# Last output tile of a projection in its own PSUM bank, squares of the other tiles summed early and folded to 256 columns

## What is computed

```python
def rms_norm(x, g):
    y = xf * lax.rsqrt(jnp.mean(xf * xf, axis=-1, keepdims=True) + EPS)
    return (y * g).astype(x.dtype)

x = x + rms_norm(y, attn_post_g[layer])     # y is the output of w_o (layers 0 and 1)
h = rms_norm(x, ffn_pre_g[layer])
f = swiglu(h, w_gate, w_up, w_down)
x = x + rms_norm(f, ffn_post_g[layer])
...
mod = silu(c) @ w_ada + b_ada               # third layer: six vectors of 1024
x = x + gt_m * mixed                        # then rms_norm(x, g_ffn), modulated
x = x + gt_f * y                            # then the final rms_norm
```

## Time and profile before

| what | value |
|---|---|
| median of 3 runs | 1028.64 us (1028.03 to 1035.65) |
| the profiled execution's own time | 1028.55 us |
| its span, first to last instruction | 1026.4 us |
| mean granted clock of PE | 0.992 of full |

### The profile page before, as it was taken

The page is one execution under the profiler, slowest core; times in us unless marked ns, Lnnn a source line. Parts: engine busy times, 40 slices in busy tenths (PEclk is TensorE's granted clock), DMA queues, the critical chain, the costliest instruction groups (busy, mean ns, idle before and its releaser), DMA issues.

```text
span 1026.4 us, 18901 instructions
## 1 busy us (share of the span) xinstructions
PE 979.2 (95%) x8022; PEld 941.3 (92%) x8022; DVE 710.8 (69%) x1248; ACT 530.1 (52%) x805; POOL 16.4 (2%) x48
## 2 busy tenths in 40 slices
PE   6978999999999999899999999998999999999996
PEld 6968989999998987789999999897999999999996
DVE  5946587787648776688867766546553877878753
ACT  6634474444337455464434443546665456666631
POOL 0000000000000000000000000000120000000000
PEclk9999999999999999999999999999999999999998
DMA  7432556667753733347775873453333544555541
GB/s 278 175 123 83 205 219 235 245 237 259 281 209 129 283 124 123 125 169 285 260 265 202 340 289 121 173 197 121 120 131 123 198 152 155 196 185 186 174 155 42
DMA packets 28307, 194.19 MB, mean 189 GB/s; under 512 B 3264, under 2 KB 3520, under 8 KB 5312
## 3 DMA queue, kind: packets, MB, share of 16 engines
q1 hardware_dynamic: 28224, 192.99, 51.9%
HBM read 191.93 MB, written 1.05 MB: 188 GB/s over the span
## 4 chain that ended last, share of the span: by engine, by line
PE 64%; DVE 17%; ACT 14%; issue 3%; DMA 1%; SPq 1%; POOL 0%; DVEq 0%; ACTq 0%
PE bank L479 17%; PE bank L480 17%; PE bank L481 17%; ACT s_whi L851 7%; DVE s_wlo L1245 4%; DVE s_tmp L1703 2%; PE bank L599 2%; DVE s_tmp L1705 2%; PE bank L524 2%; PE bank L525 1%; PE bank L530 1%; PE bank L579 1%; ACT s_tmp L1205 1%; ACT s_tmp L1201 1%; ACT s_S L895 1%
## 5 line engine op out<-in xcount | busy, mean ns | idle before, releaser
L1245 DVE TENSOR_TENSOR s_wlo<-s_raw,s_whi 128x512 fp32r<-128x512 f32 (+1 forms) x352 | 370.4, 1092 | 160.8 <-ACT s_whi L851 160.6
L851 ACT ACTIVATE s_whi<-s_raw 128x1024 fp32r<-128x1024 f32 (+2 forms) x223 | 303.1, 1387 | 237.0 <-PE bank L481 218.6
L479 PE MATMUL bank<-s_hh,s_whi 128*128 128x256 f32 x1400 | 394.5, 282 | 5.9 <-DVE s_wlo L1245 3.5
L480 PE MATMUL bank<-s_hl,s_whi 128*128 128x256 f32 x1400 | 389.2, 278 | 0.0
L481 PE MATMUL bank<-s_hh,s_wlo 128*128 128x256 f32 x1400 | 389.1, 278 | 0.0
L479 PEld LDWEIGHTS bank<-s_hh,s_whi 128*128 128x128 f32 x1400 | 263.8, 188 | 12.6 <-issue 8.6
L481 PEld LDWEIGHTS bank<-s_hh,s_wlo 128*128 128x128 f32 x1400 | 264.4, 189 | 0.0
L480 PEld LDWEIGHTS bank<-s_hl,s_whi 128*128 128x128 f32 x1400 | 264.0, 189 | 0.1
L479 PE MATMUL bank<-s_ph,s_whi 128*128 128x256 f32 x528 | 147.0, 278 | 0.6 <-DVE s_wlo L1245 0.6
L481 PE MATMUL bank<-s_ph,s_wlo 128*128 128x256 f32 x528 | 146.9, 278 | 0.0
L480 PE MATMUL bank<-s_pl,s_whi 128*128 128x256 f32 x528 | 146.9, 278 | 0.0
(11 more groups left out here) (202 smaller groups left out, 1278.2 us busy)
## 6 DMA issues: line engine op xcount, KB each, us to landing
s_raw<-in_gu SPq DMA_DIRECT2D x44, 1024.0 KB, 4.9
s_raw<-in_dn SPq DMA_DIRECT2D x33, 1024.0 KB, 4.8
s_raw<-in_wada SPq DMA_DIRECT2D x24, 1024.0 KB, 5.3
s_raw<-in_up SPq DMA_DIRECT2D x22, 1024.0 KB, 4.8
s_raw<-in_wo SPq DMA_DIRECT2D x8, 1024.0 KB, 4.8
s_raw<-in_win_g SPq DMA_DIRECT2D x8, 1024.0 KB, 4.7
s_raw<-in_wkv_v SPq DMA_DIRECT2D x4, 1024.0 KB, 5.9
s_raw<-in_wkv_k SPq DMA_DIRECT2D x4, 1024.0 KB, 4.8
```

The source lines that it names most:

```text
L479: e.matmul(out, hi, xh[:, k, :], start=first, stop=False, skip_group_check=True)
L480: e.matmul(out, hi, xl[:, k, :], start=False, stop=False, skip_group_check=True)
L851: e.activation(whi[w % SPLIT][:, at], raw[p % RAW][:, at], ACT.Copy).then_inc(S.hi.tick((w, c0)), 1)
L1245: e.tensor_tensor(wlo[s][:, at], raw[p % RAW][:, at], whi[s][:, at].bitcast(F32), ALU.subtract).then_inc(S.lo.tick((i, j), (i, "all")), 1)
```

## The change

Three things change.

1. `tiles` takes a bank `seven`. In four calls (`dn0` and `dn1` in `feed_forward` with bank 7, `wout` with bank 3, `dn2` with bank 5) the last output tile, number 7, goes to the first half of that bank; tile 6 stays in the old one and gets an event of its own, "six". ACT squares tile 6 and tile 7 in instructions of 128x256 (`last_squares`), DVE adds the squares of tile 6 to the accumulator, and at x5 and x6 it also does the gated add of tile 6 on "six".
2. DVE adds the two halves of the accumulator (`fold`, 128x256), so that PE needs one call over it and not two. With tile 6 in the accumulator, only tile 7 is late: one call, not two.
3. At y0 and y1, which get no bank of their own, PE sums the late pair first (two calls) and the folded accumulator behind it (one call).

`sums("x4")` gives the same eight calls as before, and `ada_sums(0, 7)`, `ada_sums(2, 7)` and the `keep_warm` calls are not edited. The core of the diff:

```diff
+        def tile_out(name, j):
+            if j == 7 and (name, "seven") in bank_of:
+                return banks[bank_of[name, "seven"]][:, 0:T]
+            return banks[bank_of[name, j - j % 2]][:, (j % 2) * T:(j % 2 + 1) * T]
...
-            def tiles(name, n, m, nk, xh, xl, made, b, by, last=0):
+            def tiles(name, n, m, nk, xh, xl, made, b, by, last=0, seven=None):
                 out = take(b, by, (name, n + last))
+                outs = [out[:, j * T:(j + 1) * T] for j in range(m)]
                 bank_of[name, n] = b
+                if seven is not None:
+                    outs[1] = take(seven, by, (name, n + last))[:, 0:T]
+                    bank_of[name, "seven"] = seven
...
+                        event = (name, n) if j == m - 1 else (name, "six") if seven is not None else None
...
+                if acc and s not in ("y0", "y1"):
+                    summed()
+                    for half in range(acc):
...
                 for i, src in late:
                     q.wait_ge(S.square, (s, i))
...
+                    m = e.matmul(out[:, 0:T], ones[:, :], src, start=first, stop=True, skip_group_check=True)
+                    first = False
+                if s in ("y0", "y1"):
+                    summed()
+                    m = e.matmul(out[:, 0:T], ones[:, :], sq[:, 0:T], start=False, stop=True, skip_group_check=True)
...
                 for n in (2, 4, 6):
-                    tiles(d, n, 2, NF, ph[layer], pl[layer], f"p{layer}", n // 2, S.resid, 1)
-                sums(f"z{layer}", 4, late=[(3, sq_late)])
+                    tiles(d, n, 2, NF, ph[layer], pl[layer], f"p{layer}", n // 2, S.resid, 1, 7 if n == 6 else None)
+                sums(f"z{layer}", 4, late=[(3, sq_late[:, 1, :])], acc=1)
...
+            def last_squares(s, j, src, into):
+                if j == 0 and ("sq", into) in sq_free:
+                    q.wait_ge(*sq_free["sq", into])
+                sq_free["sq", into] = (S.sums, s)
+                e.activation(sqb[into][:, j, :], src, ACT.Square).then_inc(S.square.tick((s, ("six", 3)[j])), 1)
...
+            def fold(s):
+                acc = sqacc[ACC_OF[s]]
+                q.wait_latest(S.sqsum)
+                e.tensor_tensor(acc[:, 0:T], acc[:, 0:T], acc[:, T:2 * T], ALU.add).then_inc(
+                    S.sqsum.tick((s, "sum")), 1)
...
+                    if t == 160:
+                        fold(s)
+                        square_sum(s, "six", sqb[3][:, 0, :], T)
...
             def add_gated(name, s, n, gate0):
                 for j in range(2):
+                    if j == 1 or n < 6:
+                        q.wait_ge(S.gemm, (name, n))
+                    else:
+                        q.wait_ge(S.gemm, (name, "six"))
...
+                    elif n == 6:
+                        i.then_inc(S.resid.tick((s, "six")), 1)
+                        fold(s)
+                        square_sum(s, "six", sqb[1][:, 0, :], T)
```

More of the change, by code:

```diff
@@ L545, in tokens, with sums, summed @@
                         token_low(name, g, nk, xl, k, tb)
[L547 removed]
+            def sums(s, b, late=(), acc=2, columns=False):
                 out = take(b, S.act_tmp, ("log", s))
                 bank_of["sums", s] = b
[L551 to L553 removed]
+                sq, first = sqacc[ACC_OF.get(s, 0)], True
+                def summed():
                     q.wait_ge(S.square, (s, 0))
@@ L684, in tensor_program @@
                     values("o0", A0, i, P, A0.PT[i % 2], ("wuv", i // 2, 1), S.soft, ("o0", "turned", i, 1), 7)
-            sums("y0", 4, late=[(3, sqb[1])])
+            sums("y0", 4, late=[(3, sqb[1][:, j, :]) for j in range(2)])
             keep_warm(8, 7)
@@ L743, in tensor_program @@
                     values("o1", A1, i, 64, A1.PT[i % 2], ("wkv_v", i // 4, 1), S.soft, ("o1", "turned", i, 1), 7)
-            sums("y1", 4, late=[(3, sqb[1])])
+            sums("y1", 4, late=[(3, sqb[1][:, j, :]) for j in range(2)])
             keep_warm(8, 7)
@@ L748, in tensor_program @@
             keep_warm(12, 6)
-            sums("x4", 5, late=[(i, sqb[i]) for i in range(4)], acc=False)
+            sums("x4", 5, late=[(i, sqb[i][:, j, :]) for i in range(4) for j in range(2)], acc=0)
             keep_warm(6, 6)
@@ L812, in tensor_program @@
             for n in (4, 6):
-                tiles("wout", n, 2, 8, hh, hl, "mix", (6, 7)[n // 2 - 2], S.resid)
-            sums("x5", 0, late=[(3, sqb[1])])
+                tiles("wout", n, 2, 8, hh, hl, "mix", (6, 7)[n // 2 - 2], S.resid, seven=3 if n == 6 else None)
+            sums("x5", 0, late=[(3, sqb[1][:, 1, :])], acc=1)
             keep_warm(7, 3)
@@ L828, in tensor_program @@
             for n in (2, 4, 6):
-                tiles("dn2", n, 2, NF, ph[2], pl[2], "p2", n // 2, S.resid)
-            sums("x6", 4, late=[(3, sqb[1])])
+                tiles("dn2", n, 2, NF, ph[2], pl[2], "p2", n // 2, S.resid, seven=5 if n == 6 else None)
+            sums("x6", 4, late=[(3, sqb[1][:, 1, :])], acc=1)
         def scalar_program(e, counted):
@@ L935, in y_squares @@
                         square(s, 0, bank[:, :], None, (S.sums, s))
-                    elif i < 3:
+                    else:
                         square(s, i, pair(bank), ring[i - 1], (S.sqsum, (s, i)))
-                    else:
-                        square(s, 3, pair(bank), ring[2], (S.sums, s))
                     yield i
+                if (name, "seven") not in bank_of:
+                    q.wait_ge(S.gemm, (name, 6))
+                    square(s, 3, pair(banks[bank_of[name, 6]]), ring[2], (S.sums, s))
+                else:
+                    for j, done in ((0, "six"), (1, 6)):
+                        q.wait_ge(S.gemm, (name, done))
+                        last_squares(s, j, tile_out(name, 6 + j), ring[2])
+                        yield 3
+            def last_squares(s, j, src, into):
[3 more added lines that the diff above has]
+                e.activation(sqb[into][:, j, :], src, ACT.Square).then_inc(S.square.tick((s, ("six", 3)[j])), 1)
             def x_squares(s, ring):
@@ L1170, in x_pair_squares @@
             def x_pair_squares(s, i, ring):
[L1171 to L1174, removed]
-                else:
-                    square(s, i, src, ring[i - 1], (S.sums, s) if i == 3 else (S.sqsum, (s, i)))
+                if i < 3:
+                    q.wait_ge(S.resid, (s, 2 * i))
+                    src = xT[:, 2 * i:2 * i + 2, :]
+                    square(s, i, src, *((None, (S.sums, s)) if i == 0 else (ring[i - 1], (S.sqsum, (s, i)))))
+                else:
+                    for j, done in ((0, "six"), (1, 6)):
+                        q.wait_ge(S.resid, (s, done))
+                        last_squares(s, j, xT[:, 6 + j, :], ring[2])
             hi_all(_used_up("wout", 16) + SPLIT)
```

26 lines of the change are left out of this document (11 added, 15 removed).

## The result

| what | before | after |
|---|---|---|
| median | 1029.84 us (4 runs, 1028.03 to 1035.65) | 1059.89 us (4 runs, 1058.86 to 1063.08) |
| the profiled execution: its own time, its span | 1028.55, 1026.4 | 1063.08, 1061.0 |
| mean granted clock of PE | 0.992 | 0.976 |

The ratio is 1.0287, with an interval of 1.0239 to 1.0335: slower by 30 us, where 18.5 was forecast. The profiled execution is the slowest of the four, so its time is read piece by piece here and not as a whole.

What follows compares the result with a forecast made beforehand. PE, busy 979.2 of 1026.4 us, was taken to bound the kernel. Terms at the ends summed to +15.3 us, plus 3.2 for the clock: +18.5, so 1047.0 us, with an 8-in-10 range of 1042.5 to 1051.0.

Steps and rivals of the forecast that it cites:

- The waits: At z0 and z1, PE's ada_sums waits for bank 7 until DVE adds tile 7: about 10.3 and 8 us.
- +9.8: At z0, the products of wkv_v start 9.8 us later because ada_sums waits for bank 7.
- +7.5: At z1, the Ln of x4 comes 7.49 us later because ada_sums waits for bank 7.
- The small terms: Savings: 0.6 us at y0 and y1, 0.65 at z0 and z1, 1.06 at x6; loss: 0.27 at x5.
- The cover of the fold at z1: At z1, DVE's sum of tile 6 and fold finish before PE wants the accumulator, hidden by 0.2 us.
- I take 1.6 twice: After the waits at z0 and z1, work at the low clock costs 1.6 us each, 3.2 us together.
- the upper bound of 3.0: Most the low clock could cost after each wait, from the 5.9 us at the kernel's start.
- 15.3: Sum of all terms at the ends, waits and savings together, without the clock: +15.3 us.
- the wait costs nothing: Rival: tile 7's add is done when PE reaches ada_sums, so only savings remain, 1025.3 us; 3%.
- z0 is caught up: Rival: ACT and DVE get ahead during z0's wait and PE waits less at attention, 1035.6 us; 7%.
- the clock is back at once: Rival: the clock never falls, or returns at once when PE restarts after the waits, 1043.8 us; 12%.
- the low clock of the start's length: Rival: after each wait the clock stays low as long as at the start, 3.0 us each, 1049.8 us; 18%.

Runs made afterwards that it cites:

- kernel with dummies in the gap: Changed kernel plus 40 dummy matmul calls ahead of ada_sums(0) and 32 ahead of ada_sums(2), in free bank 6: 1051.58 us, ratio 1.0168.
- the wait alone: Kernel before, with only ada_sums(0) and ada_sums(2) moved to bank 3, held until add_normed adds tile 7: 1066.29 us, ratio 1.0313.
- the wait at z1 alone: Changed kernel with a free bank for ada_sums(0) only, so PE still waits at z1: 1042.36 us, one run.
- The experiments with dummies: Changed kernel with dummy matmuls before PE's waits at z0 and z1 (1051.58 us), or between each wait and ada_sums (1058.32 us).
- the kernel with the bank freed: Changed kernel with ada_sums(0) and ada_sums(2) in banks nobody holds, three bank numbers elsewhere adjusted: 1031.86 us, ratio 0.9981 to the kernel before.

## Why the prediction was wrong

**The waits were right.** Places, releaser and lengths came as worked out ahead: 10.34 and 7.97 us, against about 10.3 and 8. The terms +9.8 and +7.5 stand, by the restart 0.06 us after the last add, and by 8.2 us at z1 in the kernel with dummies in the gap.

**The small terms were right.** By the starts of the last product and of the Ln, y0 gave 0.61 (0.6 ahead) and y1 0.66 (0.6), z0 and z1 0.65 and 0.66 (0.65), x6 1.05 (1.06), and x5 lost 0.20 (0.27). The cover of the fold at z1 held: PE took the folded sum (line 574) 0.19 us after it began the last product, and the late call still came right behind ACT's square.

**The step that failed is the price of the clock: "I take 1.6 twice".** It measured 5.6 and 5.7, and even the upper bound of 3.0 was under it: 11.3 us in place of 3.2. That the clock would fall, and that the work behind each gap would start at the low level, was right. Wrong was for how long: 12 us of PE's work, not 3.4, and not the 5.9 of the start either. In the other two kernels that wait in this way it was 12.2 and 9.6 us (the wait alone) and 10.9 (the wait at z1 alone), at prices of 5.5, 4.6 and 5.2 us: never near 1.6, though not one fixed figure. I chose the stretches nearest in place, behind shorter gaps, and did not ask what work came out of them. In those, PE went on for the most part with products, and at the start too. Here the first thing behind both gaps is `ada_sums`, and it did 6.8 us of it at 0.50 with no sign of a rise. With dummies ahead of it the clock was back after some 5 us, near the start's 5.9. The experiments with dummies show both halves of this: take the low clock away at z1 and the whole price goes; change what PE does first and the price falls from 5.7 to 2.3 (12.22 - 9.96). With this term as measured the sum is 15.3 + 11.3 = 26.6, so 1055.2.

**What is left.** The measured difference is 30.0. The kernel before took 1033.41 and 1031.61 as the medians of two sets of 17 runs, so the four runs beside the changed kernel caught it some 2 to 4 us short; as far as these medians show, that part of the miss is chance. Against 1032.5, the middle of the two, the changed kernel loses 27.4, though it was not run beside them. In its profiled execution there was a further stretch at 0.51, right behind x5, from 862.8 to 866.2; the 24 records of the first products behind the Ln ended 0.76 us later there than in the kernel before. The other kernels with the same x5 show no such stretch in their profile, so I count it to chance, not to the change. So the terms close to within about 1 us, but the medians can't bear that out: the interval of the changed kernel's loss is 24.6 to 34.5 us, and the kernel with the bank freed came out between 5.6 us under and 1.7 us over the kernel before, where the savings alone make 3.4 under. A further mechanism of a few us is not excluded by the totals; the stages compared above show none.

**The rivals.** That the wait costs nothing fell with the list of waits. That z0 is caught up fell twice: the 16 us between the Ln of z0 and of x2 are still there at x3 (446.76 before, 467.40 after: 20.64, against 20.93 at x2), and the kernel with the wait at z1 alone takes some 17 us less, in its one run. That the clock is back at once fell with 7.09 us for `ada_sums`. The rival nearest to what happened was the low clock of the start's length, with 18%; it, too, was too short by half. The Trainium skill's rule that the throttled clock is the default state and that activity releases it ("TensorE: Matmul & The Clock Gate", "What's actually happening") agrees with both gaps. Which activity, it was for the rows to say: here 6.79 of 6.80 us of PE's busy time in `ada_sums` released nothing.

**The range.** Its upper end of 1051.0 rested on 3.0 us for each stretch. The rows showed two lengths of low stretches, both behind other work than this, and I took the longer for a bound. Nothing in the trace made it one. Nor were the lengths settled: they came from a single profile, and other executions had 6.7 us at a place where it had 3.4.

## What to carry to other kernels

Before a tile moves to another bank, go through the list of who takes that bank next, and on what event it comes free: the gain here was 3.4 us at six ends, and one bank number, taken too early by side work, cost 29 to 30 at the two places where PE waited. Give side work that fills a gap a bank whose holder is done, or put it where the event has passed anyway. And if an engine has to stand still for long, price the clock by what it does first when it starts again, with a bound from the whole of that work and not from stretches behind other gaps. Take more than one profile for it.

## What the runs showed of the hardware

**The clock did not come back during `ada_sums`.** Its 32 records, 128x64 each, kept PE busy for 6.79 of 6.80 us at z0 in the changed kernel with the granted clock at 0.50, and the clock rose only 5.1 us into the products behind them. In all five places where `ada_sums` came first behind a long wait, the clock rose after it had ended, 2.7 to 5.4 us into the work that followed, and never during it. In the kernel with dummies in the gap it fell during `ada_sums`, while PE was busy for 2.50 of 2.50 us. Yet `ada_sums` right behind the end of z0, in the kernel with the bank freed, ran at 1.00 throughout. I had taken "busy" in the profile for what brings the clock back. What it is in this work that differs (the size of its calls, or something else) was not tried by itself. That it is `ada_sums` which does not bring the clock back is thus read from the order of work, not from a test of its parts.

**PE has two paces at the same granted clock.** In long runs of products a matmul starts 113.2 to 113.6 ns after the one before, or 117.8, both with the granted clock at 1.00. Here is one run of each from the timeline of the changed kernel:

```profile
309.33 0.28 PE L485 MATMUL bank<-s_ph,s_whi 128*128 128x256 f32 x1
...
309.92 0.28 PE L487 MATMUL bank<-s_ph,s_wlo 128*128 128x256 f32 x1
...
642.99 0.28 PE L485 MATMUL bank<-s_ph,s_whi 128*128 128x256 f32 x1
...
643.56 0.28 PE L487 MATMUL bank<-s_ph,s_wlo 128*128 128x256 f32 x1
```

Five steps take 0.59 us in the first and 0.57 in the second. A pace mostly holds for a whole stage and changes where PE pauses, but not always: in the kernel with the bank freed, between 877 and 939 us, five runs of products change from 118 to 113 ns half way, with no pause. In the two further profiles of the kernel before, the stage from x1 to z0 was at 113.2 in one and at 117.8 in the other, and in each of them later stages had the other pace. That stage has some 1490 product matmuls, and 4.5 ns each are 6.7 us; it varied between 171.5 and 178.1. The spans of the two profiles are 1025.0 and 1035.8 us. By the same count, the stages in which their paces differ make up some 11 us, and the low stretch that only the faster had takes 1.6 off again. It is likely most of the spread of the kernel's other runs, too (1026.7 to 1038.6), but those have no profile. It is why a saving of 3 us can be read at the ends and hardly in the total. What sets the pace was not found.
